# Adding the experts' outputs in memory, one zeroed row per token, in a decoder layer with a mixture of experts

## The reference

```python
u = x * (1.0 + scale2) + shift2
y_moe = _hier_moe(u, ...)            # for each token: sum over its 2 experts of wts * expert(u)
x = _layer_norm(DEEPNORM_ALPHA * x + gate2 * y_moe, ln_g[1], ln_b[1])
```

## Time and profile before

| | us |
|---|---|
| median of 3 runs | 1905.53 (1901.12 to 1906.41) |
| the profiled execution | 1910.53 |
| its span, from the first to the last instruction | 1908.8 |
| last stage in it, from the first load's issue | 1793.47 to the end |

### The profile page before, as it was taken

The page is one execution under the profiler, slowest core; times in us unless marked ns, Lnnn a source line. Parts: engine busy times, 40 slices in busy tenths (PEclk is TensorE's granted clock), DMA queues, the critical chain, the costliest instruction groups (busy, mean ns, idle before and its releaser), DMA issues. The chain is left out here.

```text
span 1908.8 us, 29069 instructions
## 1 busy us (share of the span) xinstructions
PE 1732.3 (91%) x8892; PEld 1341.6 (70%) x8893; DVE 1162.1 (61%) x1880; ACT 619.7 (32%) x770; POOL 585.8 (31%) x679
## 2 busy tenths in 40 slices
PE   5999999999999999999689999269999999999674
PEld 2777777777888799999468877246776776776321
DVE  3676666666666666666456887744565333455298
ACT  2333333223333322222211111123565334465233
POOL 0122222111222222012144556532443333343155
PEclk7999999999999899999799999579999999999897
DMA  6443334443333231322565342379899865797595
GB/s 251 160 135 128 113 120 144 134 144 110 97 105 94 72 100 51 101 95 58 177 196 175 128 138 100 100 239 342 295 380 361 283 217 176 267 323 289 215 390 176
DMA packets 171432, 342.72 MB, mean 180 GB/s; under 512 B 18932, under 2 KB 109844, under 8 KB 166335
## 3 DMA queue, kind: packets, MB, share of 16 engines
q1 hardware_dynamic: 148518, 285.35, 44.5%
q0 software_dynamic: 18000, 55.87, 8.0%
q10 hardware_dynamic: 4818, 0.26, 0.2%
HBM read 276.86 MB, written 64.58 MB: 179 GB/s over the span
## 5 line engine op out<-in xcount | busy, mean ns | idle before, releaser
L1532 DVE TENSOR_TENSOR w_gu_lo<-w_gu_raw,w_gu_hi (+1 forms) x64 | 146.5, 2292 | 146.9 <-ACT w_gu_hi L1525 141.7
L860 DVE TENSOR_TENSOR w_lo<-w_raw,w_hi 128x1024 fp32r<-128x1024 f32 x112 | 138.6, 1241 | 137.0 <-ACT w_hi L539 134.3
L651 POOL TENSOR_TENSOR o_r<-o_ms,neg_half 128x4 f32<-128x4 f32 (+1 forms) x16 | 16.8, 1051 | 640.6 <-DVEq L914 640.6
L685 PE MATMUL pr<-ua_hi,w_hi 128*128 128x512 f32 x448 | 185.0, 413 | 10.8 <-DVE ua_lo L865 10.8
L1920 PE MATMUL py<-w_dn_w,hhT 128*128 x400 | 183.2, 601 | 11.0 <-ACT hhT L1745 6.5
L685 PE MATMUL pr<-ub_hi,w_hi 128*128 128x288 f32 (+1 forms) x672 | 189.2, 335 | 0.0
L1881 PE MATMUL ph<-w_gu_hi,x_hi 128*128 (+1 forms) x408 | 183.4, 449 | 2.5 <-DVE x_lo L1784 2.5
L685 PE MATMUL pr<-ub_lo,w_hi 128*128 128x288 f32 (+1 forms) x672 | 183.8, 327 | 0.0
L685 PE MATMUL pr<-ub_hi,w_lo 128*128 128x288 f32 (+1 forms) x672 | 183.6, 327 | 0.0
L685 PE MATMUL pr<-ua_lo,w_hi 128*128 128x512 f32 x448 | 178.8, 399 | 0.0
L685 PE MATMUL pr<-ua_hi,w_lo 128*128 128x512 f32 x448 | 178.7, 399 | 0.0
(11 more groups left out here) (334 smaller groups left out, 3432.4 us busy)
## 6 DMA issues: line engine op xcount, KB each, us to landing
w_raw<-in_w_in SPq DMA_DIRECT2D x112, 512.0 KB, 4.1
w_gu_raw<-in_w_e_gate SPq DMA_DIRECT2D x32, 1024.0 KB
w_gu_raw<-in_w_e_up SPq DMA_DIRECT2D x32, 1024.0 KB
w_dn_w<-in_w_e_down SPq DMA_DIRECT2D x32, 1024.0 KB
w_mod<-in_w_mod_rest SPq DMA_DIRECT2D x16, 1024.0 KB
y_t<-y_scratch SPq DMA_DIRECT2D x16, 1024.0 KB, 7.5
w_ring<-in_w_mod_first SPq DMA_DIRECT2D x4, 2048.0 KB, 16.4
x_cols<-in_x_prompt_t SPq DMA_DIRECT2D x32, 256.0 KB, 4.9
```

Of the source, the lines that this page charges most:

```text
L651: pool.tensor_tensor(o_r[:, 0:c], o_ms[:, 0:c], keep["neg_half"][:, 0:c], ALU.pow).then_inc(o_rs, 1)
L685: last = pe.matmul(pr[n % 2][:, a * 512:a * 512 + c], w[:, n % WS, k, :], x[:, k, a * c:(a + 1) * c], start=(k == 0 and m == 0), stop=(k = ...
L860: dve.tensor_tensor(w_lo[:, n % WS], w_raw[:, n % WRAW], w_hi[:, n % WS].bitcast(F32), ALU.subtract).then_inc(lo_done, 1)
L1532: dve.tensor_tensor(w_slot(keep["gu_lo"], s, lo, hi), w_slot(keep["gu_raw"], r, lo, hi), w_slot(keep["gu_hi"], s, lo, hi).bitcast(F32), AL ...
```

## The change

`y2` has one row per token in place of two. The rows are set to zero during the first stage: VectorE clears `w_mod` once, at the end of unit 9, and SyncE stores zeros from it in 18 pieces, three in each of units 10 to 15. In the expert stage the scatter adds to the row in memory (`compute_op=ALU.add`). The last stage loads one row per token (0.5 MB a tile), eight tiles ahead; TensorE and ScalarE's `residual` are gone from it. VectorE multiplies the loaded tile by the gate, and computes `z` from the loaded `x1` by one `scalar_tensor_tensor`.

```diff
--- before.py
+++ after.py
@@ -359,6 +359,7 @@
...
         mod_in, mod_prod, mod_part, mod_sum = sem("mod_in"), sem("mod_prod2"), sem("mod_part"), sem("mod_sum")
+        zero_rdy, zero_out = sem("zero_rdy"), sem("zero_out")
         mod_rows, mod_out = sem("mod_rows"), sem("mod_out")
@@ -423,6 +424,7 @@
...
+        zeros = w_mod[:, :, :].rearrange("p k n -> p (k n)")[:, 0:D]
         MOD_N = 4 * D // MC
@@ -477,6 +479,11 @@
...
                     sp.dma_start(scr["mod"][:, i * MC:(i + 1) * MC], mod_r).then_inc(mod_out, 16)
+
+                def clear_sums(i):
+                    n = min(P, NTOK + P - i * P)
+                    sp.wait_ge(zero_rdy, 1)
+                    sp.dma_start(scr["y2"][i * P:i * P + n, :], zeros[0:n, :]).then_inc(zero_out, 16)
@@ -502,6 +509,9 @@
...
                             load_w(n)
+                    if u >= MOD_UNITS + 2:
+                        for i in range(3 * (u - MOD_UNITS - 2), 3 * (u - MOD_UNITS - 1)):
+                            clear_sums(i)
                     if u:
@@ -528,6 +538,7 @@
...
                 sp.wait_ge(s1_out, 16 * HEADS)
+                sp.wait_ge(zero_out, 16 * 3 * (UNITS - MOD_UNITS - 2))
@@ -1116,6 +1127,8 @@
...
                     convolve(u)
+                    if u == MOD_UNITS + 1:
+                        dve.memset(zeros, 0.0).then_inc(zero_rdy, 1)
                 last_u = UNITS - 1
@@ -1302,8 +1315,8 @@
...
                 pool.iota(R["rows"][:, :, 1, 0], pattern=[[P, T]], base=0, channel_multiplier=1)
-                pool.iota(R["rows"][:, :, 0, 1], pattern=[[2 * P, T]], base=0, channel_multiplier=2)
-                pool.iota(R["rows"][:, :, 1, 1], pattern=[[2 * P, T]], base=1, channel_multiplier=2)
+                pool.iota(R["rows"][:, :, 0, 1], pattern=[[P, T]], base=0, channel_multiplier=1)
+                pool.iota(R["rows"][:, :, 1, 1], pattern=[[P, T]], base=0, channel_multiplier=1)
                 pool.memset(R["rows"][:, :, :, 3], 0)
@@ -1488,7 +1501,7 @@
...
                         dve.drain()
-                        dve.tensor_scalar(fill[:, :, 1], slot_i[:, :], 2 * NTOK, None, ALU.add)
+                        dve.tensor_scalar(fill[:, :, 1], slot_i[:, :], NTOK, None, ALU.add)
                         dve.drain().then_inc(fill_rdy, 1)
@@ -1709,7 +1722,8 @@
...
                         wait_apart(pool, y_out, 16 * g, tick)
-                    pool.indirect_dma_start(scr["y2"], bass.IndirectOffsetOnAxis(ap=ids_cur[:, half, 1:2], axis=0), y_sb[:, half, :], None).then_inc(y_out, 16)
+                    pool.indirect_dma_start(scr["y2"], bass.IndirectOffsetOnAxis(ap=ids_cur[:, half, 1:2], axis=0), y_sb[:, half, :], None,
+                                            compute_op=ALU.add).then_inc(y_out, 16)
@@ -1929,14 +1943,14 @@
...
     LAST = T - 1
-    R = 6
+    R = 8
     with ExitStack() as ctx:
...
         x1 = sb("x1_t", [P, R, D])
-        y2 = sb("y2_t", [P, R, 2, D])
+        y2 = sb("y2_t", [P, R, D])
         zw = sb("zw4", [P, D])
@@ -1947,13 +1961,11 @@
...
         nmean = sb("nmean4", [P, 2])
-        ps_y = [ps("ps_y0", [P, D]), ps("ps_y1", [P, D])]
-        ps_x = ps("ps_x4", [P, D])
         ps_n = ps("ps_n4", [P, D])
...
         o_out = [sem("o_out%d" % s) for s in range(4)]
-        ysum, weighed, xa_rdy, z_rdy, var_rdy, off_rdy, zn_rdy, zg_rdy, o_rdy, fin_rdy = (
-            sem(n + "4") for n in ("ysum", "weighed", "xa_rdy", "z_rdy", "var_rdy", "off_rdy", "zn_rdy", "zg_rdy", "o_rdy", "fin_rdy"))
+        weighed, z_rdy, var_rdy, off_rdy, zn_rdy, zg_rdy, o_rdy, fin_rdy = (
+            sem(n + "4") for n in ("weighed", "z_rdy", "var_rdy", "off_rdy", "zn_rdy", "zg_rdy", "o_rdy", "fin_rdy"))
         op, os_ = outs[0][0], outs[1].rearrange("b l d -> (b l) d")
@@ -1965,9 +1977,9 @@
...
                     if t >= R:
-                        sp.wait_ge(ysum, t - R + 1)
-                        sp.wait_ge(xa_rdy, t - R + 1)
-                    sp.dma_start(y2[0:n, s, :, :], scr["y2"][t * 2 * P:t * 2 * P + 2 * n, :].rearrange("(p k) d -> p k d", k=2)).then_inc(in_[s], 16)
+                        sp.wait_ge(weighed, t - R + 1)
+                        sp.wait_ge(z_rdy, t - R + 1)
+                    sp.dma_start(y2[0:n, s, :], scr["y2"][t * P:t * P + n, :]).then_inc(in_[s], 16)
                     sp.dma_start(x1[0:n, s, :], scr["x1"][t * P:t * P + n, :]).then_inc(in_[s], 16)
@@ -1989,13 +2001,6 @@
...
             def _(act):
-                def residual(t):
-                    n = rows_of(t)
-                    act.wait_ge(in_[t % R], 32 * (t // R) + 32)
-                    if t:
-                        act.wait_ge(z_rdy, t)
-                    act.activation(ps_x[0:n, :], x1[0:n, t % R, :], ACT.Copy, scale=ALPHA).then_inc(xa_rdy, 1)
-
                 def centre(t):
@@ -2003,12 +2008,8 @@
...
-                residual(0)
-                for t in range(T):
-                    if t:
-                        centre(t - 1)
-                    if t + 1 < T:
-                        residual(t + 1)
+                for t in range(LAST):
+                    centre(t)
@@ -2037,30 +2038,16 @@
...
-            @block.tensor
-            def _(pe):
-                for t in range(T):
-                    n, s = rows_of(t), t % R
-                    pe.wait_ge(in_[s], 32 * (t // R) + 32)
-                    if t >= 2:
-                        pe.wait_ge(weighed, t - 1)
-                    for k in range(2):
-                        for hf in range(2):
-                            last = pe.matmul(ps_y[t % 2][0:n, hf * 512:(hf + 1) * 512], keep["ident"][0:n, 0:n],
-                                             y2[0:n, s, k, hf * 512:(hf + 1) * 512], start=(k == 0), stop=(k == 1))
-                    last.then_inc(ysum, 1)
-
             @block.vector
...
                     n = rows_of(t)
-                    dve.wait_ge(ysum, t + 1)
-                    dve.tensor_tensor(zw[0:n, :], ps_y[t % 2][0:n, :], (gate_s if n < P else gate_p)[0:n, :], ALU.mult).then_inc(weighed, 1)
+                    dve.wait_ge(in_[t % R], 32 * (t // R) + 32)
+                    dve.tensor_tensor(zw[0:n, :], y2[0:n, t % R, :], (gate_s if n < P else gate_p)[0:n, :], ALU.mult).then_inc(weighed, 1)
...
                     n, h = rows_of(t), t % 2
-                    dve.wait_ge(xa_rdy, t + 1)
-                    dve.tensor_tensor(z[0:n, h, :], ps_x[0:n, :], zw[0:n, :], ALU.add)
+                    dve.scalar_tensor_tensor(z[0:n, h, :], x1[0:n, t % R, :], ALPHA, zw[0:n, :], ALU.mult, ALU.add)
                     dve.drain().then_inc(z_rdy, 1)
@@ -2250,7 +2237,7 @@
...
         "list": nc.dram_tensor("list_scratch", [(NE + 1) * CAP, 4], I32).ap(),
-        "y2": nc.dram_tensor("y2_scratch", [2 * NTOK + P, D], F32).ap(),
+        "y2": nc.dram_tensor("y2_scratch", [NTOK + P, D], F32).ap(),
     }
```

## The result

The changed kernel takes 1951.22 us (median of 4 runs, 1943.68 to 1958.97), the kernel before 1905.44 (4 runs, 1901.12 to 1906.41): a ratio of 1.0249, with a 95% interval of 1.0224 to 1.0274. The forecast was 1951. The profiled execution of the changed kernel is its fastest one, 1943.68 us with a span of 1942.1, so its terms add up to less than the medians do: +33.3 us of span.

A forecast was written before the change was run, and what follows sets the result against it. TensorE was taken to bound the expert stage, with weights late in one-block stretches, and VectorE the last stage; 22.3 (last stage) + 21 (destination reads) + 2 (last scatter) = 45 on 1905.5 gave 1951 us, range 1922 to 1990.

The forecast's parts named there:

- turn-taking: Last stage: VectorE's `z`, with both tiles in SBUF, waits for GpSimd's `o_t` addition; 1.95 us a tile, 29.3 us in all.
- The start of the stage: Last stage: TensorE's 5.71 us of sums go and the first loads land 1.4 us earlier; 7 us gained.
- The destination read: Expert stage: each adding scatter also reads its destination rows, 1.30 us more DMA time a block, delaying weights; +21 us.
- The wait after the last scatter: From expert stage to last stage: the read ahead of the last scatter's write lengthens the 7.05 us wait; +2 us.
- Rival C: Expert stage: the scatter's landing becomes the bound, period 12.4 us instead of 10.01, total 2050 us; chance 0.19.
- the forecast's limit: Expert stage: the next scatter isn't late while a landing takes under 8.0 us; 7.8 was expected, fitting barely.
- Rival B: Expert stage: the destination read is hidden, only the tail and the last stage cost; 1929 us; chance 0.22.
- D: Last stage: GpSimd's addition doesn't hold `zw` and `z`, 7 us won; 1900.5 us, or 1921 with full-price read; chance 0.06.
- The zeros: First stage, units 9 to 15: eighteen stores and one fill are hidden; cost 0, or 1.2 us without cover.

The follow-up runs named there:

- an operand out of SBUF: Changed kernel with `zw` in PSUM, so `z` reads one tile from SBUF and one from PSUM: 1919.21 us, ratio 1.0073.
- GpSimd's work away: Changed kernel with the bias `ln_b` left out of the first 16 tiles of the last stage, ScalarE copying `zg` to `o_t`: 1922.54 us, ratio 1.0090.
- the line alone in the old kernel: Kernel before, with only `z` computed from `x1` and `zw`, both in SBUF, in place of `ps_x` and `zw`: 1922.80 us, ratio 1.0087.
- the plain scatter: Changed kernel with a scatter that overwrites instead of adding, so each token keeps one expert's output: 1925.03 us, ratio 1.0099.
- The run with a read in place of the addition: Changed kernel with an overwriting scatter, and beside each block a plain load of 0.52 MB into an unused tile: 1952.84 us, ratio 1.0251.

## Why the prediction was right

- *The bound and the main step, turn-taking: right, in mechanism and size.* The forecast was `z` at 3.2 us and a tile at 7.6; the profile has 3.19 and 7.54. It was read off one instruction of the kernel before, `o_t` of the last tile in the earlier trace rows, whose neighbours stand in the same order. Three runs test it from three sides: an operand out of SBUF (-32.0 us), GpSimd's work away (-28.7), the line alone in the old kernel (+17, forecast from the same turn-taking with another order). By the Trainium skill (SBUF — State Buffer, Who interferes with whom) either of the first two should free `z`; both did (1.22 and 1.23 us). 15 x 1.89 = 28.4 us, against 29.3 forecast.
- *The start of the stage: right.* -7.35 us, forecast -7.
- *The destination read: the sum right, two of its terms not, so the sum in part by luck.* Forecast +21; the means of the profiled stages differ by 22.2, the changed kernel's own profile has 12.7, and the plain scatter takes 26.2 from the whole with the tail. The read was priced at 1.30 us of the DMA engines. A lone scatter takes 2.19 more than before (3.49 against 1.30). Over the whole run the queue's total rose by 11.9% of 1942.1 less 8.0% of 1908.8, 78 us, or 1.57 a scatter (the read beside a plain one: 1.40). So the price was too low, alone and under load. What a price costs TensorE was taken too high in return: at 1.57 us the forecast's own sum would give about 28 us. It charged 1300 to 1340 with 5.2 us, and there TensorE is busy 40.00 of 40 us as before, at a share of 1.04; why it lost nothing wasn't tested (weights are loaded three experts ahead). It charged 1380 to 1480 with 13 us, where the same scatters took 9.3 us longer. The halving that the Trainium skill gives for transfers that add in a collective (Collectives: The Full Stack, Why ReduceScatter is half of AllGather) is milder than what the lone scatter shows here (2.7 times the engines' time).
- *The wait after the last scatter: mis-sized.* +3.7 us, forecast +2, of which 0.6 are the longer issue on GpSimd, which the forecast didn't have at all.
- *Rival C, the landing: its condition came true, its consequence did not.* By the trace, 23 of the changed kernel's 50 scatters landed 9.0 us or more after their issue began, the longest 10.8; with an issue of 1.61 us the forecast's limit is 7.4 us behind the issue, 9.0 from its start. One scatter's issue ended at 1365.87, and the next started at 1374.11, 8.2 us later, after waiting for it. Yet from 1487.98 to 1680.51 the scatters follow each other every 10.13 us on average (10.02 before), between 8.2 and 13.0 apart: a late one is made up for by the next. The rule that a landing over the limit sets the period was too strict. The run with a read in place of the addition loses as much with hardly a late landing.
- *Rival B, a hidden read, and D, no turn-taking:* refuted, B by the plain scatter, D by the three runs on the last stage.
- *The zeros: right* within what the runs can tell: 0.1 us between the runs with and without the stores. The longest wait for `w_raw` in the second half of the first stage is 14.7 us before and after.

Sum of the measured terms: 28.4 - 7.35 + 22.2 + 3.7 = 47, and 45.8 us are between the medians. The 22.2 is the difference of means over several kernels. With the changed kernel's own 12.7 the terms come to 37, and its profile has 33.3 us, since 3.3 were gained before the first scatter by chance of the execution.

## What to carry to other kernels

Before moving an operand of a VectorE instruction from PSUM to SBUF, look what GpSimd runs beside it: here, with two tiles in SBUF, the two engines took turns, and the work that TensorE and ScalarE did on the way to PSUM was what had kept them apart. If the detour is to go, let VectorE's own intermediate stand in PSUM; that was a change of one word here and took back 32 us, though it left the kernel 0.7% slower than before. An addition in the DMA wasn't free here, where transfers already filled the engines: it moved a sum from a stage in which TensorE had time to one in which the DMA engines had none.

## What the runs showed of the hardware

- An adding indirect scatter of 128 rows of 4 KB takes 3.49 us of all 16 DMA engines alone, where the plain one takes 1.30; GpSimd issues it in 1.61 us in place of 1.01.
- Adding scatters landed 6.0 to 10.8 us after their issue began in the expert stage; the one behind the last block landed after 6.1, and the next stage started 5.6 us after that.
- Its reads of the destination don't appear in the profile's packets, bytes or HBM reads (18000 packets and 55.87 MB on queue 0 with and without); the busy share shows them.
- TensorE has no work in the last stage, and its granted clock there is 0.50 (1.2 GHz; the row of 1810 to 1942 us above). Nothing waits for it, but it pulls down the mean over the span, 0.927 in place of 0.949, which a reader could take for a throttled kernel.
